# Fused mixer and MoE block on one core: quarter matmuls in the last level of the delta rule's block inverse, the meta inverse moved beside the substitution, first attention by pairs of heads

## What is computed

```python
q, k, v = conv, silu, l2norm of the projections          # 8 heads of 128
A = where(tri_strict, (k*beta) @ k.T * decay, 0)          # per head and chunk
Tm = triangular_solve(A + eye, eye)                       # the inverse of a unit lower triangle
u, w = Tm @ (v*beta), Tm @ (k*beta*exp(gc))               # then the scan over chunks
y_gdn = rmsnorm(o) * silu(z)
# second branch: for each block of 128 queries, 64 keys are chosen by an index score
p = softmax(where(chosen, q @ k.T * ATT_HD**-0.5, -inf)); y_dsa = p @ v   # 8 heads, 2 kv heads
merged = sigmoid(gate_a) * (y_gdn @ w_bg) + sigmoid(gate_b) * (y_dsa @ w_bd)
```

## Time and profile before

| | |
|---|---|
| median of 3 runs | 1258.56 us |
| the profiled execution | 1259.38 us |
| its span | 1257.6 us |
| TensorE busy, weight loads busy | 1191.4 us (95%), 1027.9 us (82%) |
| VectorE, ScalarE, GpSimd busy | 667.8, 502.1, 83.9 us |
| TensorE's mean granted clock | 0.976 of full |
| read from HBM | 252.19 MB |

### The profile page before, as it was taken

The page is one execution under the profiler, slowest core; times in us unless marked ns, Lnnn a source line. Parts: engine busy times, 40 slices in busy tenths (PEclk is TensorE's granted clock), DMA queues, the critical chain, the costliest instruction groups (busy, mean ns, idle before and its releaser), DMA issues.

```text
span 1257.6 us, 21686 instructions
## 1 busy us (share of the span) xinstructions
PE 1191.4 (95%) x9068; PEld 1027.9 (82%) x9068; DVE 667.8 (53%) x1161; ACT 502.1 (40%) x809; POOL 83.9 (7%) x80
## 2 busy tenths in 40 slices
PE   7999779999899989999998999999899899999996
PEld 6998669998879969999997889966799866666665
DVE  5776685487966565664646332576556441122223
ACT  4775322554355455554344222466533301011112
POOL 2541113000000000000000000000001100000000
PEclk8999889999999999999998999999999899999999
DMA  9546030153422655554554522300865989999980
GB/s 363 189 146 243 13 135 1 68 172 130 163 106 101 239 198 212 191 188 165 184 186 154 196 101 71 132 33 6 326 234 219 387 365 420 420 420 420 420 346 34
DMA packets 36206, 254.61 MB, mean 202 GB/s; under 512 B 4048, under 2 KB 4192, under 8 KB 5904
## 3 DMA queue, kind: packets, MB, share of 16 engines
q1 hardware_dynamic: 33552, 237.83, 49.1%
q0 software_dynamic: 2560, 15.42, 3.1%
HBM read 252.19 MB, written 1.05 MB: 201 GB/s over the span
## 4 chain that ended last, share of the span: by engine, by line
PE 87%; DVE 9%; ACT 2%; issue 2%; DMA 0%; DVEq 0%; ACTq 0%
PE bank L1255 14%; PE bank L676 12%; PE bank L670 12%; PE bank L671 12%; PE bank L632 9%; PE bank L1016 5%; PE bank L1065 4%; PE bank L1023 2%; PE bank L714 1%; PE bank L1274 1%; PE bank L689 1%; PE bank L787 1%; PE bank L802 1%; DVE ring_low L1923 1%; DVE rB L1904 1%
## 5 line engine op out<-in xcount | busy, mean ns | idle before, releaser
L1923 DVE TENSOR_TENSOR ring_low<-ring,w_high 128x2048 fp32r<-128x2048 f32 x104 | 237.9, 2289 | 175.5 <-ACT w_high L1475 175.2
L1475 ACT ACTIVATE w_high<-ring 128x2048 fp32r<-128x2048 f32 x104 | 199.4, 1917 | 311.7 <-PE bank L676 222.3
L670 PE MATMUL bank<-nT_high,w_high 128*128 128x256 f32 (+1 forms) x448 | 115.3, 296 | 0.0
L670 PEld LDWEIGHTS bank<-nT_high,w_high 128*128 128x128 f32 x448 | 85.0, 190 | 2.6 <-issue 2.4
L1255 PE MATMUL bank<-more,xs 128*64 128x256 f32 x768 | 84.5, 379 | 0.0
L670 PE MATMUL bank<-hcl,w_high 128*128 128x256 f32 (+1 forms) x288 | 81.9, 316 | 2.2 <-DVE hcl L2367 2.2
L1255 PEld LDWEIGHTS bank<-more,xs 128*64 128x64 f32 x768 | 55.1, 137 | 29.8 <-issue 2.9
L671 PE MATMUL bank<-hcl,w_high 128*128 128x256 f32 (+1 forms) x288 | 79.4, 307 | 0.0
L670 PE MATMUL bank<-nMs,w_high 128*128 128x256 f32 x256 | 65.2, 292 | 2.0 <-DVE nMs L2312 2.0
L671 PE MATMUL bank<-nT_low,w_high 128*128 128x256 f32 (+1 forms) x272 | 65.5, 282 | 0.0
L671 PE MATMUL bank<-nMs,w_high 128*128 128x256 f32 x256 | 64.8, 291 | 0.0
(11 more groups left out here) (542 smaller groups left out, 2490.9 us busy)
## 6 DMA issues: line engine op xcount, KB each, us to landing
ring<-stream SPq DMA_DIRECT2D x163, 1024.0 KB, 4.9
more<-stream SPq DMA_DIRECT2D x60, 1024.0 KB, 16.4
more<-stream POOLq DMA_DIRECT2D x10, 1024.0 KB, 15.3
c<-constants_one SPq DMA_DIRECT2D x1, 1653.0 KB, 16.2
qc<-h_in SPq DMA_DIRECT2D x4, 272.0 KB, 3.8
c<-constants_two POOLq DMA_DIRECT2D x1, 1056.0 KB, 9.4
beside<-stream POOLq DMA_DIRECT2D x1, 1024.0 KB, 12.2
hT<-h_in POOLq DMA_DIRECT2D x1, 1024.0 KB, 5.9
```

The source lines that it names most:

```text
L670: nc.tensor.matmul(into[j], w, high_x(k), start=first, stop=False, skip_group_check=True)
L1475: A(w_high[:, d % 2, :], ring[:, s, :], ACT.Copy).then_inc(high_ready, 1)
L1923: TT(ring_low[:, s, :], ring[:, s, :], w_high[:, d % 2, :], sub).then_inc(low_ready, 1)
```

## The change

- The last level (joining blocks of 64 rows) is done on quarters: P is a 64x64 product of the lower left quarter of `low` with the upper left quarter of the inverse, written to PSUM partitions 64 to 127; QT is 64x64 on partitions 0 to 63. No mask, ScalarE copies 64x256 elements and VectorE updates 64x256.
- The meta items leave the head loop. They stand after it, between the units `mod` 6, `mod` 7 and quarters of the two `gz` units (four matmuls of 256 columns each); VectorE's updates stand at three places of the substitution.
- The copy to `egl` and the scaling of the queries go from VectorE to POOL, in a loop between its second and third mask.
- The first attention transposes two heads into one bank (a second one for the meta keys in the second query tile) and multiplies values with 256 columns for two heads at once. `prob` has four slots. `gate_b` 1 moves into TensorE's loop at n = 8, and ScalarE and VectorE prepare a weight unit at n = 5 and at n = 13 of their loops.

```diff
@@ weight_order @@
-    for u in range(4):
+    order += [("gate_b", 0), ("gate_b", 1), ("bd", 0), ("bd", 1)]
+    for u in range(2, 4):
         order += [("gate_b", u), ("bd", u)]
@@ TensorE @@
             def level_p(n):
                 l, g = LEVEL_ITEMS[n]
+                if l == LEVELS - 1:
+                    emptied(pe, ("QT", LEVEL_ITEMS.index((l - 1, g))))
+                    dst = take(("P", n))
+                    for j, s in enumerate(systems(g)):
+                        last = nc.tensor.matmul(dst[64:128, j * 64:(j + 1) * 64], low[0:64, s, 64:128], inv[0:64, s, 0:64], start=True, stop=True)
+                    done(("P", n), last)
+                    return
...
+                if l == LEVELS - 1:
+                    for j, s in enumerate(systems(g)):
+                        last = nc.tensor.matmul(dst[0:64, j * 64:(j + 1) * 64], prod[64:128, n % 2, j * 64:(j + 1) * 64], invT[64:128, s, 64:128], start=True, stop=True)
+                    done(("QT", n), last)
+                    return
...
-                if h % 2 == 1:
-                    level_p(h // 2)
-                elif h >= 2:
-                    level_q(h // 2 - 1)
...
             mod_unit(6)
+            level_p(0)
             mod_unit(7)
-            level_q(META_LEVELS - 1)
-            for kind, u in FILLERS:
...
+            level_q(0)
+            quarter(0, 0)
+            quarter(0, 1)
+            level_p(1)
+            quarter(0, 2)
+            level_q(1)
+            quarter(0, 3)
+            level_p(2)
+            quarter(1, 0)
+            level_q(2)
+            quarter(1, 1)
+            level_p(3)
+            quarter(1, 2)
+            level_q(3)
+            quarter(1, 3)
...
-                if n == 0:
-                    second_gate(0)
+                if n % 8 == 0 and n < len(ATT):
+                    second_gate(n // 8)
                 if 1 <= n <= len(ATT):
                     att_transpose(n - 1)
-                if n >= 3:
-                    att_values(n - 3)
+                if n >= 4 and n % 2 == 0:
+                    att_values((n - 4) // 2)
@@ POOL @@
-            for n, (l, g) in enumerate(LEVEL_ITEMS):
-                if n == META_LEVELS:
+            for n, (l, g) in enumerate(LEVEL_ITEMS[:-4]):
+                if n == 2:
+                    for h in range(H):
+                        pool.wait_ge(decay_exp_ready, h + 1)
+                        pool.wait_ge(*banks.full_when[("KQ", h)])
+                        nc.gpsimd.tensor_copy(egl[:, 2 * h:2 * h + 2], scr[:, h % 2, 256:512].rearrange("p (a b) -> p a b", b=128)[:, :, 127])
+                        nc.gpsimd.tensor_tensor(qc[:, h, META:T], qc[:, h, META:T], scr[:, h % 2, 256:512], mul).then_inc(gpsimd_product, 1)
@@ ScalarE @@
                     act.wait_ge(decay_arg_ready, h + 1)
+                    if h >= 2:
+                        act.wait_ge(gpsimd_product, 24 + h - 1)
...
-                if 2 <= n < len(ATT) + 2:
...
+                if n >= 3 and n % 2 == 1 and n < len(ATT) + 3:
+                    p = (n - 3) // 2
...
+                if n >= 5 and n % 2 == 1:
+                    p = (n - 5) // 2
+                    qt, h = ATT[2 * p]
+                    evac(("ao", p), y_dsa[:, h:h + 2, qt * 128:(qt + 1) * 128], 256)
...
+                if n == 5 or n == 13:
+                    after_unit("gate_b", n // 8)
+            emptied(act, ("gate_b", 0))
+            emptied(act, ("gate_b", 1))
+            A(gate[:, :, :], gate[:, :, :], ACT.Sigmoid).then_inc(sig_ready, 1)
@@ VectorE @@
-                step(CP(egl[:, 2 * h:2 * h + 2], split(scr[:, h % 2, 256:512], 128)[:, :, 127]))
...
-                step(TT(qc[:, h, META:T], qc[:, h, META:T], scr[:, h % 2, 256:512], mul))
...
+                if l == LEVELS - 1:
+                    corner = invT[0:64, 4 * g:4 * g + 4, 64:128]
+                    TT(corner, corner, split(full(dve, ("QT", n))[0:64, 0:256], 64), sub).then_inc(free(("QT", n)), 1)
+                    return
...
-                if h >= 3 and h % 2 == 1:
-                    update_inverse(h // 2 - 1)
...
             step.settle()
+            update_inverse(0)
...
+                if j == 9:
+                    update_inverse(1)
+            update_inverse(2)
...
+                if n == 5 or n == 13:
+                    after_unit("gate_b", n // 8)
                 if n >= 1:
                     k = n - 1
                     w = nkeys(ATT[k][0])
                     dve.wait_ge(pexp_ready, k + 1)
```

More of the change, by code:

```diff
@@ L822, in _, with quarter @@
                 done(("TR", h), last)
-                if h % 2 == 1:
-                    level_p(h // 2)
-                elif h >= 2:
-                    level_q(h // 2 - 1)
+            placed = {}
+            def quarter(u, q):
+                if q == 0:
+                    placed[u] = unit("gz", u), take(("gz", u))
+                (s, cnt), dst = placed[u]
+                j, half = divmod(q, 2)
+                for k in range(half * KT // 2, (half + 1) * KT // 2):
+                    last = nc.tensor.matmul(dst[:, j * SEQ:(j + 1) * SEQ], by_k(s)[:, k, j * 128:(j + 1) * 128], nT[:, k, META:T],
+                                            start=(j == 0 and k == 0), stop=(k == KT - 1), skip_group_check=True)
+                if q == 3:
+                    last.then_inc(unit_used[s], 1)
+                    banks.full_when[("gz", u)] = (unit_used[s], cnt)
             mod_unit(6)
+            level_p(0)
             mod_unit(7)
-            level_q(META_LEVELS - 1)
-            for kind, u in FILLERS:
-                s, cnt = unit(kind, u)
-                dst = take((kind, u))
-                for j in range(2):
-                    last = group(dst[:, j * SEQ:(j + 1) * SEQ], [(by_k(s)[:, k, j * 128:(j + 1) * 128], nT[:, k, META:T]) for k in range(KT)])
-                last.then_inc(unit_used[s], 1)
-                banks.full_when[(kind, u)] = (unit_used[s], cnt)
+            level_q(0)
[13 more added lines that the diff above has]
+            quarter(1, 3)
             for n in range(META_LEVELS, len(LEVEL_ITEMS)):
@@ L1599, in _ @@
                             ins.then_inc(free(("TR", g)), 1)
-                if h >= 2 and h % 2 == 0:
-                    product_out(h // 2 - 1)
             evac_mod(6)
+            product_out(0)
             evac_mod(7)
-            for u in range(2):
-                gz_out(u)
+            product_out(1)
+            product_out(2)
+            gz_out(0)
+            product_out(3)
+            gz_out(1)
             for n in range(META_LEVELS, len(LEVEL_ITEMS)):
@@ L1656, in second_gate @@
                     emptied(act, ("bg", u + 2))
-                A(gate[:, u % 2, :], full(act, ("gate_b", u))[:, :], ACT.Copy if u == 0 else ACT.Sigmoid).then_inc(free(("gate_b", u)), 1)
+                A(gate[:, u % 2, :], full(act, ("gate_b", u))[:, :], ACT.Copy if u < 2 else ACT.Sigmoid).then_inc(free(("gate_b", u)), 1)
             first_gate(0)
@@ L1689, in _ @@
[L1689 to L1694 removed]
+                    if n == 2 or n == 11:
+                        second_gate(n // 8)
+                    if n >= 4:
+                        act.wait_ge(*banks.full_when[("pt", (n - 4) // 2)])
@@ L2266, in _ @@
                     step.settle()
[L2267 to L2270 removed]
+                    TS(prob[:, k % 4, 0:w], prob[:, k % 4, 0:w], stat[:, k % 2, 2:3], None, mul).then_inc(prob_ready, 1)
+            for p in range(H // 2):
+                dve.wait_ge(y_dsa_high_ready, p + 1)
+                TT(y_dsa_low[:, 2 * p:2 * p + 2, :], y_dsa[:, 2 * p:2 * p + 2, :], y_dsa_high[:, 2 * p:2 * p + 2, :], sub).then_inc(y_dsa_ready, 1)
             for u in range(4):
[L2272 removed]
+                if u >= 2:
+                    after_unit("gate_b", u)
                 emptied(dve, ("gate_b", u))
```

94 lines of the change are left out of this document (49 added, 45 removed).

## The result

| | before | after |
|---|---|---|
| median of the runs | 1258.96 us (11 runs, 1255.33 to 1277.78) | 1262.52 us (11 runs, 1260.52 to 1265.22) |
| profiled execution, its span | 1259.38, 1257.6 us | 1262.42, 1260.6 us |
| TensorE busy | 1191.4 us (95%) | 1189.2 us (94%) |
| VectorE, ScalarE, GpSimd busy | 667.8, 502.1, 83.9 us | 661.4, 500.6, 85.1 us |
| mean granted clock | 0.976 | 0.969 |

The ratio is 1.0035, 95% interval 1.0022 to 1.0048: 4.4 us slower (2.8 to 6.0), within the 0.5% that I had called no change. A few executions ran at a clearly lower granted clock (two of the eleven before, two in experiment 2 and one of 1514.79 us in experiment 4); they count in the medians and are left out of the ratios. The forecast was 1259.0, so it lies 3.5 us low, inside its range. Behind the small difference stand two large ones of opposite sign, as forecast.

The account below looks back on a forecast made before the run. TensorE was taken as the bound from the scan through the attention and behind it, VectorE's sequence in the head loop. Terms - 12.1 + 1.9 + 1.2 - 2.3 + 11.7 = + 0.4 gave 1259.0 us against the median, range 1246 to 1266.

Parts of the forecast that it names:

- Head loop: Delta rule's head loop: period 2.93 us instead of 3.02, meta items' waits and a held-up copy gone; minus 12.1 us.
- Updates: Meta updates inside VectorE's substitution: five more operations of 0.29 us and one wait of about 0.5; plus 1.9 us.
- the port: SBUF port shared by VectorE and POOL: one mask's full time falls into the substitution; plus 1.2 us, between 0 and 3.3.
- Last level: Last block level on quarters: passes of 0.6 us instead of 0.90; minus 2.3 us, between minus 3.2 and plus 1.1.
- Attention: First attention: savings by pairs against slower rhythm, two stalls for weight preparations and lower clock; plus 11.7 us in sum.
- rhythm: Attention: values come in lumps every second step, so logits come late and TensorE waits some 0.5 us; plus 2.3 us.
- two gaps: Attention: TensorE idles at the transposes of heads 4 and 12 while weights are prepared; plus 4.9 and 5.4 us.
- clock, net of waits that it hides: Attention: lower clock behind both stalls, partly taken up by waits of the rhythm; plus 1.7 us, between 0 and 2.2.
- The preparations are hidden: Attention: weight preparations cause no stalls, so it costs 0 instead of 11.7 us; time 1247.3 us; chance 15%.
- TensorE bounds the head loop: Head loop: the denser loop runs at the lower clock, seven heads lose 1.5 us each; plus 10, time 1269; chance 9%.
- POOL's product against the masked decay: Head loop: POOL's and VectorE's operations meet, each head pays up to 0.65 us; plus 5, time 1264; chance 12%.
- The last level at full price: Last block level: quarter passes cost as much as full ones or more; plus 3.4 us, time 1262.4; no chance given.

Follow-up runs that it names:

- experiment 2: Only the delta rule's part of the change, with the attention of the kernel before: 1248.78 us, ratio 0.9913 to the kernel before.
- experiment 4: The changed kernel with the last level again on whole 128 x 128 blocks with masks: 1267.25 us, ratio 1.0067 to the kernel before.
- experiment 1: The changed kernel with the attention loop's two weight preparations moved, one beside gate_b 1, one behind the loop: 1251.69 us, ratio 0.994 to the kernel before.
- experiment 6: The changed kernel with the copy to egl and the scaling of the queries back on VectorE: 1265.59 us, ratio 1.006 to the kernel before.
- experiment 10: The changed kernel with POOL's first mask of 512 elements held back until VectorE's last meta update: 1264.13 us in one run.
- experiment 3: Only the attention's part of the change, with the delta rule of the kernel before: 1274.55 us, ratio 1.0124 to the kernel before.
- experiment 8: The changed kernel, preparations moved, logits two heads ahead at every step, filling matmuls ahead of the first block level: 1240.96 us, ratio 0.987 to the kernel before.
- experiment 9: The delta rule's part alone, with the single-head attention of the kernel before, and logits two heads ahead: 1244.79 us, ratio 0.9892 to the kernel before.
- experiment 7: The changed kernel with preparations moved and logits of one more head issued ahead of each values group: 1247.23 us, ratio 0.9911 to the kernel before.
- experiment 5: The changed kernel with unread matmuls filling TensorE's idle time ahead of the first block level and transposes of heads 4 and 12: 1255.49 us, ratio 0.9985.

## Why the prediction was near, and where it was off

The forecast summed its terms to + 0.4; the four stages of the profiled pair sum to + 3.9. The attention accounts for + 3.75 of the error. The rest is small because a head loop 0.95 us longer than forecast was made up for by three terms that came out 1.3 us better together, and that is luck.

*Head loop, forecast - 12.1, measured - 11.2* (36.43 to 25.28; - 11.4 and - 11.8 in experiments 2 and 1). The period and the 3.90 us behind the last arguments are right to 0.05. The step "the second head's arguments stay" is what was off: the first period was 3.74 us here and 3.10 to 3.44 there, not 2.91. TensorE's matmuls for the first heads ran at the lower level here until about 124.7 us, 2.8 behind the first arguments, and before until about 125.4, 1.1 behind them. The memset came at 147.19 and not near 148.7, since this execution started 2.4 us earlier and its loop was 0.95 longer than forecast. The split was off too: I put the whole copy held up by POOL, 2.5 us, down to the move of work to POOL. Moving the meta items alone takes 1.85 us of it away (2.66 to 0.81, experiment 6).

*Updates, forecast + 1.9, measured + 1.0, and the port, forecast + 1.2, measured + 1.0.* The updates are six operations, not the five I counted, but they follow each other every 0.2 us and not every 0.29, and the first two cost 0.2 together. The wait of 0.5 for the third product was hidden by the 0.94 that the mask had cost before it; without that it appears, as 0.42 (experiment 10). For the port I took one mask and bounded it by three; it was 0.94 us beside the one mask of 512 elements that met an operation with two inputs, and 0.1 beside a small one (0.32 instead of 0.22 us). With the rule that I cited there from the Trainium skill ("SBUF — State Buffer", "Who interferes with whom") the trace agrees: both operations ended 0.07 to 0.08 us behind their mask. The transposes beside POOL's memset did not slow down (4.18 us, 4.23 before).

*Waiting and clock ahead of the levels, forecast no change:* right. TensorE was idle for 5.22 us (before 5.98), and the two passes took 3.75 again.

*Last level, forecast - 2.3, measured - 2.5* by experiment 4, inside the bounds. A lone pass takes the 0.6 forecast, but not every pass does: some overlap (0.40), and waits take part of that back, so that the sum came out near in part by luck. The argument from the weight loads was weak too: 137 of 192 ns is 0.71, hardly nearer to the half than to the whole.

*Attention, forecast + 11.7, measured + 15.45* (73.55 to 89.00), + 15.6 by the ratio of experiment 3. Here the forecast failed, and this is almost its whole error. The mechanism was right, the two gaps and a lower clock behind them; one term was too small. Its parts:

| | forecast | measured | from |
|---|---|---|---|
| values by pairs | - 2.6 | - 2.8 | experiments 8 and 9 |
| rhythm | + 2.3 | + 3.0 | experiment 1 less before, and 2.8 added; experiment 7 gave back 3.3 |
| two gaps | + 4.9 + 5.4 | + 4.85 + 5.36 | rows of after |
| clock, net of waits that it hides | + 1.7 | + 5.1 | after less experiment 1, less the gaps; 5.7 by experiment 5 |

The step that failed reads "idle of 5.98 us was followed by two passes at the lower level, plus 1.8; ... for both stalls between 0 and 2.2 I take 1.7". I took the loss behind one long wait as the price for both, and let the waits of the rhythm absorb part. The runs show a loss behind each: TensorE was at the lower level through 6.2 us behind the first gap and, with 0.65 as the mean, through 9.9 us behind the second, so that in these it did half to two thirds of what it does at full clock. The comparison with experiment 1 gives both sides: busy 75.70 against 69.22 us, + 6.5, while its waits outside the gaps shrink by 1.5 (idle 13.3 with the gaps of 10.2, against 4.6). The waits of the rhythm did absorb 1.5, as forecast; what was left of the loss was three times the 1.7 that I took. Why the lower level lasted as long as it did behind these gaps no run shows.

*Rivals.* "The preparations are hidden", 15%: no. But moved by a few steps they are (experiment 1): the whole unit that I named in favour of this rival can cover one of them, if it stands beside it. "TensorE bounds the head loop", 9%: no; the loop was granted 0.94 as the mean, and only the first period suffered. "POOL's product against the masked decay", 12%: no; it ran from 1.5 to 2.3 us behind the arguments, as in my order, and met nothing. "The last level at full price": no.

*Behind the attention* I forecast nothing; the pair shows + 1.4. The span there differs by more between kernels that are alike in it (831.0 and 833.1 us in experiments 9 and 2), so this pair cannot show a term of the change there.

## What to carry to other kernels

A gap of 5 us on TensorE where it is the bound cost more than its length here: another half of it in the attention and over a third at the block levels, in matmuls at 1.2 GHz behind it. So count gaps one by one, each with its clock, and fill or move them first. A preparation on ScalarE and VectorE that belongs beside a whole unit of matmuls has to stand, in each engine's own order, where the queue of TensorE has that unit, not at a round step of a loop; and where one engine issues a lump every second step, the small work that feeds the others goes ahead of the lump.

## What the hardware showed beyond that

- Quarter passes on different parts of the array overlap. From 196.18 to 197.38 us TensorE worked on three passes, two of P and one of QT, with their records alternating: 0.40 us a pass, against 0.59 for a lone one with quarter passes behind it (197.38 to 197.97) and 0.61 with a full one behind it. The Trainium skill ("TensorEngine Tiling (Array Packing)", Key Properties) says that different tiles can load and multiply in parallel; the trace agrees, and the forecast had not used it. At the level's end the chain over ScalarE takes part of it back (0.24 us of idle, ended by prod).
- A VectorE operation with one tensor input can be locked out by POOL too: the contiguous scaling of z took 1.20 us instead of 0.35 beside a mask (experiment 10). Transposes hardly suffered: in the changed kernel the first of the four behind it ran beside a mask, and the four took 4.31 us; the next four, without a mask, took 4.23. The Trainium skill ("SBUF — State Buffer", "Who interferes with whom") names tensor_scalar among the operations that can, under conditions, take both ports and so contend with GpSimd; the trace agrees.
- Kernels that are alike in a part still differ in it from execution to execution: by up to 3 us before the first arguments and by up to 4 behind the attention, together with the granted clock there. The four stages, where no edit touched them, stayed within 0.8 us. Effects of 1 to 2 us can be read there, and not in totals.
